# The first norm of a conditioned decoder step: squares on two engines into eight buffers, summed chunk by chunk on TensorE

## The reference

```python
def _rmsnorm(x, g):
    xf = x.astype(jnp.float32)
    y = xf * lax.rsqrt(jnp.mean(xf * xf, axis=-1, keepdims=True) + EPS)
    return (y * g.astype(jnp.float32)).astype(x.dtype)
...
    mod = (jax.nn.silu(c) @ w_ada + b_ada).reshape(bsz, N_MOD, 1, D_MODEL)
...
    x = x + HALF * gt1 * _swiglu(_rmsnorm(x, g_ffn1) * (1 + sc1) + sh1, w_ffn1_up, w_ffn1_down)
    hm = _rmsnorm(x, g_mix) * (1 + scm) + shm
...
    x = x + gtm * mix
    x = x + HALF * gt2 * _swiglu(_rmsnorm(x, g_ffn2) * (1 + sc2) + sh2, w_ffn2_up, w_ffn2_down)
```

## Time and profile before

| | us |
|---|---|
| median of 3 runs | 995.83 |
| lowest and highest of them | 995.28, 996.75 |
| the profiled execution's own time | 994.56 |
| its span, first to last instruction | 992.7 |
| PE busy | 978.7 |
| DVE, ACT, POOL busy | 676.8, 539.4, 611.0 |
| mean granted TensorE clock, as a share | 0.997 |

### The profile page before, as it was taken

The page is one execution under the profiler, slowest core; times in us unless marked ns, Lnnn a source line. Parts: engine busy times, 40 slices in busy tenths (PEclk is TensorE's granted clock), DMA queues, the critical chain, the costliest instruction groups (busy, mean ns, idle before and its releaser), DMA issues.

```text
span 992.7 us, 20132 instructions
## 1 busy us (share of the span) xinstructions
PE 978.7 (99%) x7589; PEld 940.5 (95%) x7589; DVE 676.8 (68%) x1391; ACT 539.4 (54%) x1000; POOL 611.0 (62%) x529
## 2 busy tenths in 40 slices
PE   9999999999999999999999999999999999999997
PEld 7899999999999998889986998999999999999996
DVE  3787766676666644369996547976666776667676
ACT  5756554566554542373265436665545665555663
POOL 3267676677676563346887143677666676767773
PEclk9999999999999999999999999999999999999998
DMA  9922322232224328745213622223222232223222
GB/s 371 369 85 89 124 85 86 85 117 97 85 86 169 129 86 292 268 162 211 86 34 155 271 96 76 86 86 120 92 87 86 100 114 86 86 91 123 86 86 96
DMA packets 22717, 127.52 MB, mean 128 GB/s; under 512 B 4192, under 2 KB 7392, under 8 KB 8032
## 3 DMA queue, kind: packets, MB, share of 16 engines
q1 hardware_dynamic: 19744, 105.28, 29.3%
q10 hardware_dynamic: 2880, 20.97, 5.6%
HBM read 123.06 MB, written 3.19 MB: 127 GB/s over the span
## 4 chain that ended last, share of the span: by engine, by line
PE 94%; POOL 2%; DVE 1%; ACT 1%; issue 1%; DMA 0%; DVEq 0%; POOLq 0%; ACTq 0%
PE tile_a L805 23%; PE tile_b L805 23%; PE ada_ps L805 18%; PE tile_a L640 8%; PE tile_b L640 7%; PE tile_a L778 3%; PE ada_ps L616 2%; PE tile_b L778 2%; PE tile_a L972 1%; PE tile_b L661 1%; POOL x_hi_room L2503 1%; PE ada_ps L984 1%; PE stat_ps L902 1%; PE tile_a L1047 1%; PE tile_a L690 1%
## 5 line engine op out<-in xcount | busy, mean ns | idle before, releaser
L2351 POOL TENSOR_TENSOR w_lo<-w_raw,w_hi 128x512 fp32r<-128x512 f32 (+1 forms) x177 | 225.5, 1282 | 92.5 <-ACT w_hi L1161 92.5
L2351 POOL TENSOR_TENSOR w_lo<-s_raw,w_hi 128x512 fp32r<-128x512 f32 (+1 forms) x118 | 152.6, 1294 | 73.5 <-ACT w_hi L1161 73.4
L1161 ACT ACTIVATE w_hi<-w_raw 128x512 fp32r<-128x512 f32 (+1 forms) x177 | 109.5, 620 | 64.7 <-PE ada_ps L805 52.5
L805 PE MATMUL tile_a<-x_hi,w_hi 128*128 128x288 f32 x400 | 117.8, 295 | 0.1
L805 PE MATMUL tile_a<-x_hi,w_lo 128*128 128x288 f32 x400 | 117.7, 294 | 0.0
L805 PE MATMUL tile_b<-x_hi,w_lo 128*128 128x288 f32 x400 | 117.7, 294 | 0.0
L805 PE MATMUL tile_b<-x_hi,w_hi 128*128 128x288 f32 x400 | 117.7, 294 | 0.0
L805 PE MATMUL tile_a<-x_lo,w_hi 128*128 128x288 f32 x400 | 117.7, 294 | 0.0
L805 PE MATMUL tile_b<-x_lo,w_hi 128*128 128x288 f32 x400 | 117.7, 294 | 0.0
L2309 POOL TENSOR_TENSOR w_lo<-w_raw,w_hi 128x2048 fp32r<-128x2048 f32 x13 | 59.9, 4606 | 78.7 <-ACT w_hi L1137 75.7
L805 PE MATMUL ada_ps<-x_hi,w_hi 128*128 128x288 f32 x320 | 94.2, 294 | 0.0
(11 more groups left out here) (346 smaller groups left out, 2972.6 us busy)
## 6 DMA issues: line engine op xcount, KB each, us to landing
w_raw<-w_units SPq DMA_DIRECT2D x78, 1024.0 KB, 4.8
ada_lo<-w_ada SPq DMA_DIRECT2D x16, 1024.0 KB, 7.9
ada_lo<-w_ada ACTq DMA_DIRECT2D x14, 1024.0 KB, 7.2
ada_hi<-w_ada ACTq DMA_DIRECT2D x6, 1024.0 KB, 6.4
x<-x_in SPq DMA_DIRECT2D x4, 576.0 KB, 5.6
y_out<-x SPq DMA_DIRECT2D x8, 288.0 KB, 2.5
x_lo_room<-conv_state SPq DMA_DIRECT2D x1, 480.0 KB, 11.1
conv_s_out<-x_lo_room SPq DMA_DIRECT2D x1, 480.0 KB, 4.8
```

Of the source, the lines that this page charges most:

```text
L805: mm = pe.matmul(ps, slot(w, i)[:, P * k:P * (k + 1)], r, start=(first and n == 0 and k == 0), stop=(n == 2 and k == kc - 1), skip_group_c ...
L1161: nc.scalar.activation(slot(w_hi, i, wide(u)), source, ACT.Copy).then_inc(ready, 1)
L2351: return nc.gpsimd.tensor_tensor(slot(w_lo, i, n), raw, slot(w_hi, i, n).bitcast(F32), ALU.subtract)
```

## The change

The first norm's eight squares get eight buffers, `first_sq`, which are tiles that aren't in use yet (`sq`, `full`, `mean_ab`, `sil` and a free part of `x_lo_room`). ScalarE squares the even chunks, VectorE the odd ones, by a multiply of `x` with itself, each as soon as its pair of chunks is loaded. Nothing is added on VectorE: PE's `first_sums` runs five matmuls for each of the eight chunks, all into the same five columns of `stat_ps`, and six fillers after each of the first three pairs of chunks. The first fillers are 24 and not 74, the 7 after products(0) are gone, and 16 stand behind turn(0). On ScalarE the root and the first copy move ahead of the split of the first weights. The helpers `squares_before` and `adds_before` count the semaphores of the later norms anew; nothing else changes there.

```diff
+        first_sq = [sq[:, 0, :], sq[:, 1, :], full[:, 0, :], full[:, 1, :], acc, mean_b, sil[:],
+                    x_lo_room[:, 0, X_FREE:X_FREE + TOKENS]]
...
+            def first_sums():
+
+                pe.wait_ge(consts_ready, 1)
+                for c in range(KD):
+                    pe.wait_ge(first_sq_ready[c % 2], c // 2 + 1)
+                    mm = token_sums(sums_ps, first_sq[c], c == 0, c == KD - 1)
+                    if c % 2 and c < KD - 1:
+                        keep_warm(0, 6)
+                mm.then_inc(stat_done, 1)
...
-            keep_warm(0, 74)
-            column_sums(0)
+            keep_warm(0, 24)
+            first_sums()
             first_products(0)
-            keep_warm(0, 7)
             norm_spread(0)
             keep_warm(0, 3)
             first_turn(0)
+            keep_warm(0, 16)
...
-            for c in range(KD):
-                square(0, c)
+            for c in range(0, KD, 2):
+                act.wait_ge(x_in_sem[c // 2], 16)
+                nc.scalar.activation(first_sq[c], x[:, c, :], ACT.Square).then_inc(first_sq_ready[0], 1)
+
...
             load_table(ACT.Sqrt)
+            root(0)
+            first_copy(0)
             act.wait_ge(w_raw_ready[0], 16)
             nc.scalar.activation(w_half(w_hi, 0, 0), raw_half(0, 0), ACT.Copy).then_inc(w0_half_ready, 1)
-            root(0)
             nc.scalar.activation(w_half(w_hi, 0, 1), raw_half(0, 1), ACT.Copy).then_inc(w_hi_ready, 1)
-            first_copy(0)
...
-            for c in range(KD):
-                add_square(0, c)
+            for c in range(1, KD, 2):
+                dve.wait_ge(x_in_sem[c // 2], 16)
+                nc.vector.tensor_tensor(first_sq[c], x[:, c, :], x[:, c, :], ALU.mult).then_inc(first_sq_ready[1], 1)
```

More of the change, by code:

```diff
@@ L156, in wide, with squares_before, adds_before @@
     return P * k_blocks(u)
+def squares_before(n):
+    return KD * (n - 1)
+def adds_before(n):
+    return (KD - 1) * (n - 1)
 def downs_before(u):
@@ L358, in trunk @@
         gate_tmp, x_ready = sem("gate_tmp"), sem("x_ready")
+        first_sq_ready = [sem("first_sq_act"), sem("first_sq_dve")]
         sq_ready, sq_used, stat_done, std_ready, rstd_ready = (
@@ L711, in last_down_unit @@
                         if h and k == n // 2:
-                            pe.wait_ge(sq_used, (KD - 1) * 4)
+                            pe.wait_ge(sq_used, adds_before(4))
                             final_sums(0, acc, True, False)
@@ L730, in final_norm @@
                 final_sums(1, acc, True, False)
-                pe.wait_ge(sq_ready, KD * 4)
+                pe.wait_ge(sq_ready, squares_before(4))
                 final_sums(1, sq[:, 1, :], False, True).then_inc(stat_done, 1)
@@ L880, in partial_sums @@
                 pe.wait_ge(consts_ready, 1)
-                pe.wait_ge(sq_used, (KD - 1) * (n + 1))
+                pe.wait_ge(sq_used, adds_before(n + 1))
                 token_sums(sums_ps, acc, True, False)
             def column_sums(n):
-                if n == 0:
-                    partial_sums(0)
-                else:
-                    pe.wait_ge(sq_half_ready, n)
-                    token_sums(sums_ps, sq[:, 1, :], False, False, 0, 2)
-                    if n < 3:
-                        fillers(n, 8)
-                pe.wait_ge(sq_ready, KD * (n + 1))
-                token_sums(sums_ps, sq[:, 1, :], False, True, 2 if n else 0).then_inc(stat_done, 1)
+                pe.wait_ge(sq_half_ready, n)
+                token_sums(sums_ps, sq[:, 1, :], False, False, 0, 2)
+                if n < 3:
+                    fillers(n, 8)
+                pe.wait_ge(sq_ready, squares_before(n + 1))
+                token_sums(sums_ps, sq[:, 1, :], False, True, 2).then_inc(stat_done, 1)
+            def first_sums():
[6 more added lines that the diff above has]
+                mm.then_inc(stat_done, 1)
             def token_sums(out, part, first, last, begin_block=0, end_block=TOKEN_BLOCKS):
@@ L1248, in square @@
             def square(n, c):
-                if n == 0:
-                    act.wait_ge(x_in_sem[c // 2], 16)
-                elif n == 3 and c < KD - 2:
+                if n == 3 and c < KD - 2:
                     d = fast_downs_before(FFNS[1][LAST_PART][3] + c // 2) + 1
@@ L1264, in square @@
                 if c >= 2 + n // 3:
-                    act.wait_ge(sq_used, (KD - 1) * n + c - 1)
+                    act.wait_ge(sq_used, adds_before(n) + c - 1)
                 nc.scalar.activation(sq[:, c % 2, :], x[:, c, :], ACT.Square).then_inc(sq_ready, 1)
             def last_square(n):
-                act.wait_ge(sq_used, (KD - 1) * n + KD - 2)
+                act.wait_ge(sq_used, adds_before(n) + KD - 2)
                 act.wait_ge(x_half_ready, n)
@@ L1293, in final_squares @@
             def final_squares():
-                act.wait_ge(sq_used, (KD - 1) * 3 + KD - 2)
+                act.wait_ge(sq_used, adds_before(3) + KD - 2)
                 act.wait_ge(x_half_ready, 3)
@@ L1707, in add_square @@
                 if 0 < c < KD - 1:
-                    dve.wait_ge(sq_ready, KD * n + c + 1)
+                    dve.wait_ge(sq_ready, squares_before(n) + c + 1)
                 if n == 3 and 0 < c < KD - 1:
                     if c > 1:
-                        dve.wait_ge(sq_used, (KD - 1) * n + c)
+                        dve.wait_ge(sq_used, adds_before(n) + c)
                     out = by_half(acc) if c == KD - 2 else acc_ps
```

## The result

The change makes the kernel slower, by 1.45%: 1010.62 us is the median of 4 runs (1009.8 to 1012.15), against 995.94 us of before in the same session (995.28 to 996.75). The ratio is 1.0145, its 95% interval 1.0133 to 1.0157. The forecast was 1008.0, with a range up to 1010.0: the direction was right and the clock fell in the sums as forecast, but the size was 2.6 us short, and the median lies 0.6 us above the range. The profiled execution took 1010.52 us, with a span of 1008.2, where before had 994.56 and 992.7.

What follows compares the result with a forecast made beforehand. TensorE, busy 978.7 of 992.7 us, bounds the kernel; products(2) 12.9 later, 4.1 of it at full clock, gives 1007.5 against the profiled execution, 1008.7 against the median. Forecast 1008.0, from 1005.5 to 1010.0; 8-in-10 range 998.8 to 1010.0.

Steps and rivals of the forecast that it cites:

- Squares, adds, the table's load: hidden: First norm: what VectorE and ScalarE save, and ScalarE's table load, hide behind PE's sums; a VectorE square taken as 0.8 us.
- A plain f32 sum is two instructions; 80 of them in the queue: First norm on PE: each sum's five matmuls run as ten, 20 per pair; six more tiles add 6.9 us.
- Prices at the full clock: +4.1: Start of products(2) at full clock: 4.1 us later than 20.84, 3.1 for the sums and 1.0 for the fillers.
- The clock falls in the sums, and a sum then takes twice as long: First norm: clock falls at 10.8, a sum goes from 0.115 to 0.22 us, the sums end at 24.6.
- Taken as at the start, where it came after 4.5 us, the clock is back at 29.1.: Behind products(0): full clock returns at 29.1 us, giving products(1) at 31.2 and products(2) at 33.7, 12.9 later than 20.84.
- ScalarE's split and GpSimd's low parts: still hidden: First weights: split late behind products(0), low parts done by 33.0 us, ahead of the unit chunk at 34.7; no cost.
- SyncE: no cost: Weight loads: products(0) free their slot later, but block 3 lands at 25 to 26 us against a need at 28.
- Nothing behind products(2) gives time back: After products(2): PE's steps of 3.14 us stay the bound, and a 99% busy PE has no wait to absorb the loss.
- The base: Starting time for the added loss: the profiled execution, 994.56 us, gives 1007.5; the median, 995.83, gives 1008.7.
- the clock holds: Rival for the first norm: only added sums and fillers are paid, 999.9 us (998.8 to 1001.2); chance 0.31.
- would be over by 2 to 3 us: Aside on the first 24 fillers: if transposes don't raise the clock, the forecast is too high by 2 to 3 us.
- sums keep their pace at the low clock: Rival for the first norm: clock falls but sums stay at 0.115 us, ending at 19.2; 1002.6 us; chance 0.13.

Runs made afterwards that it cites:

- the second trace: The changed kernel run once more, unedited, with a trace of its own: 1011.57 us, median of 4, ratio 1.0156 to before.

## Why the prediction had the direction right, and where it failed

- **Squares, adds, the table's load: hidden.** Right. A square on VectorE takes 0.76 us (0.8 taken); all is done at 10.84, and PE doesn't need it before 22.5.
- **A plain f32 sum is two instructions; 80 of them in the queue.** Right: x20 for each pair.
- **Prices at the full clock: +4.1.** Too high by 1.0. The 24 fillers ended at 6.55 and not at 7.0, and a sum has a pitch of 0.105 when start is taken to start, not the 0.115 that the 20 sums of before had. Measured is 3.1 (wide matmuls between the sums).
- **The clock falls in the sums, and a sum then takes twice as long.** Right, and the point on which it was decided. The fall came at 9.14 and not at 10.8, since the 3.8 us taken from the end of the kernel were 2.6 here (and 4.2 behind 44 fillers); the pitch was 0.21 and not 0.22. Together with the earlier start this put the end of the sums at 24.70, where 24.6 was forecast: two misses that cancel.
- **"Taken as at the start, where it came after 4.5 us, the clock is back at 29.1."** This is the step that failed: a return at a fixed delay of 4.5 us behind the start of products(0), carried over from the first fillers. It came back at 33.04, 8.3 us after products(0) began. The four us between are 16 fillers, 3.6 us instead of 1.9, and what stands around them. Products(1) came at 32.90 and not at 31.2, products(2) at 35.45 and not at 33.7. So the term that was mis-sized is the low clock's: 11.5 us instead of 8.8. The runs show that no fixed delay would have been right: with the same instructions behind products(0) it was 8.1 us once and 12.3 us once, and 3.3 us in before with 24 fillers. In the five traces of the 80 sums with at most 6 fillers after a pair and nothing wide between them, the return stands at 32.8 to 33.7, wherever products(0) begin (21.2 to 25.8). Why there stays open. The range allowed for a fall 1 or 2 us sooner or later, but for no spread of the return.
- **ScalarE's split and GpSimd's low parts: still hidden.** Right. The low parts were forecast for 33.0 and came at 32.8; the unit chunk, forecast for 34.7, starts at 36.45, 1.00 behind the start of products(2) as in before (20.84 and 21.84).
- **SyncE: no cost.** Right. In the first steps PE waits for no transfer, and they are 3.14 apart.
- **Nothing behind products(2) gives time back.** Right in sign. By the starts of its products the changed kernel is 15.1 us late at 388 us and 15.7 from this row on, which has a wait that the trace of before hasn't; the second trace has 14.6 and 14.9 at these places.

```profile
406.21 1.07 PE L629 MATMUL ada_ps<-ada_lo,cond 128*32 128x256 f32 x16 [0.49 <-DMA ada_lo<-w_ada]
```

  So 0.2 to 1.1 us may be added further on, and it differs from one execution to the next. By medians the loss is 14.7 (1010.62 - 995.94) and 14.9, the 14.6 to 14.7 of products(2).
- **The base.** The forecast was set between a sum against the profiled execution (1007.5) and one against the median (1008.7). The median was the right base: 995.83 + 14.7 = 1010.5. Of the 2.6 us by which the forecast was short, 1.7 are the sum (14.6 where it gave 12.9) and 0.7 this choice.

Of the rivals, "the clock holds" was the one to fear, with 999.9. It did not happen with one-column sums and fillers, but the run with wide matmuls shows that its price list was right but for 1 us. The aside that without a rise under the first fillers the forecast "would be over by 2 to 3 us" has no working. By the prediction's own prices the 28 sums and 6 fillers ahead of 10.8 would then take 3.9 us longer, so the forecast would be too low. The first fillers did raise the clock. That sums keep their pace at the low clock is refuted by the rows of x20, 2.29 us and 4.27. The Trainium skill, page "TensorE: Matmul & The Clock Gate", section "LDWEIGHTS (loading the stationary operand)", gives a load as its columns over 1.2 GHz, with one value for both levels; for 128 columns that is an estimated 107 ns. The pitch of the sums agrees at the full clock (0.108) and disagrees at the low one (0.21).

## What to carry to other kernels

A sum over partitions with the data as weights and one column of ones costs 0.1 us an instruction at the full clock, about what a 128x128 transpose costs, and in this kernel a queue of 80 of them lost the full clock for all that followed up to 33 us as well, though PE is busy throughout. If partial results come sooner than PE can take them, add them on the engine that is idle anyway, or stream them past stationary ones, and look at the granted clock before you look at busy time. When a low clock is forecast, price the return as widely as the fall, and don't hang it on a delay behind the work that you think brings it: that delay was 3.3 to 12.3 us here. The forecast took 4.5, and the low clock cost 11.5 us and not 8.8; a term that depends on the return needs a range of that size.

## What the runs showed of the hardware

- A long queue of one-column f32 matmuls without wide ones among them loses the full clock, even back to back: in the changed kernel 2.6 us after they began. With four instructions of 288 columns ahead of every ten but the first, 80 of them left it at 1.00 in the traced execution. Fillers, which are transposes of 128x128, don't hold it: 6 for every 20 sums did not, and 24 for every 20 gave a clock that goes up and down. Forty sums with 6 fillers for every 10 kept it to their end, and it fell 0.7 us behind them.
- The clock can fall far from an edit. Kernels with a differing start but the same instructions in the second norm had a fall there (547 to 550 us, 1.55 us) or had none. The kernel before itself ranged from 994.56 us, with a mean clock of 0.997, to 999.46, with 0.992, on one chip. A few tenths of a per cent between two versions may be that alone.
- VectorE's reciprocal is dear: 1.95 us for 128x288, where a multiply of twice the size (128x576) takes 0.76.
- A VectorE instruction with both inputs in SBUF took 2.43 us in place of 0.75 beside one of GpSimd's, and ended 0.55 us behind it; with one input in PSUM it took 0.75. The same trace has it once more: 1.21 us from 26.10 on, again 0.55 behind GpSimd's end (26.76).
